# Routed experts of a two-layer mixer model: blocks of 32 places in four column groups instead of 64 in two

## What is computed

```python
N_EXPERTS = 64; TOP_K = 8; EXPERT_HIDDEN = 256; D_MODEL = 1024
def moe_ffn(t, router_w, router_bias, w1, w3, w2, sw1, sw3, sw2):
    scores = jax.nn.sigmoid(tf @ router_w)
    _, idx = lax.top_k(scores + router_bias, TOP_K)
    gate = ROUTED_SCALE * gate / jnp.sum(gate, -1, keepdims=True)
    ...
    def expert_block(acc, blk):
        tok, g, e = blk
        xb = t_ext[tok]
        hb = jax.nn.silu(xb @ w1[e]) * (xb @ w3[e])
        return acc.at[tok].add((hb @ w2[e]) * g[:, None]), None
    ...
    shared = (jax.nn.silu(tf @ sw1) * (tf @ sw3)) @ sw2
    return acc[:n_tok] + shared
```

## Time and profile before

| | us |
|---|---|
| median of 3 runs | 2253.8 (2253.52 to 2259.19) |
| the profiled execution, its own time | 2257.79 |
| its span, first to last instruction | 2256.0 |
| routed experts of layer 0 on PE | 624.3 to 1204.5 |
| routed experts of layer 1 on PE | 1661.7 to 2201.1 |

### The profile page before, as it was taken

How to read it: one execution, slowest core, us unless ns; L and a number is a source line. 1 busy time by engine, 2 the same in 40 slices (tenths; PEclk the granted TensorE clock), 3 DMA queues, 4 the chain that set the end, 5 groups by cost and what they waited for, 6 DMA issues and landing times. The chain is left out here.

```text
span 2256.0 us, 31768 instructions
## 1 busy us (share of the span) xinstructions
PE 1924.1 (85%) x10720; PEld 984.6 (44%) x10721; DVE 847.4 (38%) x1771; ACT 287.6 (13%) x566; POOL 655.2 (29%) x948
## 2 busy tenths in 40 slices
PE   6999988976799989999996797696689878877894
PEld 2333344734455445555553333244455444443442
DVE  0224458834623223333331737433443222222224
ACT  2123354112000000000001200201100000000001
POOL 1000000000356546666661000000056444434430
PEclk9999999998799999999998899798799999989997
DMA  8655410131489999989993560405369999999935
GB/s 353 259 213 215 170 39 0 68 158 50 194 338 411 412 414 404 388 339 411 388 365 163 231 233 28 186 0 220 130 255 408 413 413 413 413 412 410 408 137 205
DMA packets 99717, 601.65 MB, mean 267 GB/s; under 512 B 23120, under 2 KB 23227, under 8 KB 40188
## 3 DMA queue, kind: packets, MB, share of 16 engines
q1 hardware_dynamic: 64396, 499.67, 54.6%
q0 software_dynamic: 35248, 100.98, 12.1%
HBM read 590.50 MB, written 51.92 MB: 285 GB/s over the span
## 5 line engine op out<-in xcount | busy, mean ns | idle before, releaser
L1737 PE MATMUL bank<-moe_w,blk_xT 128*64 128x256 f32 x5632 | 683.7, 398 | 0.0
L1737 PEld LDWEIGHTS bank<-moe_w,blk_xT 128*64 128x64 f32 x5632 | 406.7, 143 | 219.7 <-issue 33.4
L1748 PE MATMUL bank<-moe_w,xt 128*64 128x512 f32 x1408 | 332.1, 592 | 1.5 <-DVE xt L1825 1.5
L1664 POOL DMA_INDIRECT ada_rows<-v_tokens,blk_gidx x264 | 272.5, 1032 | 140.8 <-issue 135.4
L1813 DVE STREAM_TRANSPOSE blk_xT<-ada_rows 128x512 f32<-128x512 f32 x132 | 94.0, 712 | 454.3 <-PE bank L1737 434.6
L494 PE MATMUL bank<-moe_w,xt 128*128 128x512 f32 x544 | 246.2, 609 | 14.0 <-DMA moe_w<-in_odd_w_in 9.7
L1680 POOL DMA_INDIRECT y_rows<-xt,blk_sidx x176 | 180.0, 1023 | 96.5 <-issue 53.8
L1796 ACT ACTIVATE xt<-bank 128x128 f32<-128x128 f32 x174 | 48.3, 278 | 1057.3 <-PE bank L1737 1057.3
L1832 DVE COPY xt<-bank 128x512 f32<-128x512 f32 x176 | 121.8, 692 | 149.3 <-PE bank L1748 149.3
L494 PEld LDWEIGHTS bank<-moe_w,xt 128*128 128x128 f32 x544 | 104.0, 195 | 150.3 <-issue 138.5
L1748 PEld LDWEIGHTS bank<-moe_w,xt 128*64 128x64 f32 x1408 | 101.1, 137 | 127.4 <-issue 100.5
(11 more groups left out here) (382 smaller groups left out, 1651.6 us busy)
## 6 DMA issues: line engine op xcount, KB each, us to landing
moe_w<-in_experts SPq DMA_DIRECT2D x128, 3072.0 KB, 31.5
moe_w<-in_ada_w POOLq DMA_DIRECT2D x20, 2048.0 KB
moe_w<-y_rows SPq DMA_DIRECT2D x24, 1024.0 KB, 20.2
moe_w<-in_even_w_in SPq DMA_DIRECT2D x8, 2048.0 KB, 8.5
moe_w<-in_odd_w_in SPq DMA_DIRECT2D x7, 2048.0 KB, 12.6
moe_w<-in_ada_w SPq DMA_DIRECT2D x4, 2048.0 KB, 14.5
ada_rows<-v_tokens,blk_gidx POOLq DMA_INDIRECT x264
moe_w<-in_even_w_out SPq DMA_DIRECT2D x1, 4096.0 KB, 13.8
```

The lines of the kernel that those rows point to most:

```text
L1664: pool.indirect_dma_start(came[q][:, u], None, v_quarters, bass.IndirectOffsetOnAxis(ap=gidx[q][:, u:u + 1], axis=0), bounds_check=4 * n_t ...
L1737: last = nc.tensor.matmul(g.bank[1][64 * h:64 * h + 64, 0:HID], xT[:, k], w[:, s, (2 * k + h) * HID:(2 * k + h + 1) * HID], start=k == 0, ...
L1748: last = nc.tensor.matmul(g.bank[3][64 * h:64 * h + 64, :], hT[:, 64 * m:64 * m + 64], w[:, s, at:at + 512], start=m == 0, stop=m == 1)
```

## The change

Blocks have SB = 32 places. The 128 partitions now hold four quarters of 32 places each, in the gathered tile as in the result.

- `up_project` runs 8 x 4 = 32 matmuls: stationary 128x32, moving 128 columns, in four column groups. `down_project` runs 2 x 4 = 8: stationary 128x32, moving 256 columns. The weights are laid out for this on the host; their size is the same.
- `hidden` is 128x64, and DVE turns it in 32x32 squares straight into `hT`; the transpose on PE and the copy from bank 2 are gone. PE has a wait with a semaphore increment in its place.
- A block has one gather (128 rows of 1 KB) and one scatter (128 rows of 1 KB). Both take their row numbers from the two columns of one tile `places`, which DVE fills (`list_places`, one copy of 128x2 each turn); POOL copies nothing.
- DEPTH is 6: six `came`, `y` and `places` tiles, and the total of blocks is rounded up to a multiple of 6. Scatters run LAG = 3 blocks behind. From the counts: 161 blocks, run as 162, in layer 0, and 100, run as 102, in layer 1: 264 turns.
- `routing_stage` compares with 32 slots instead of 64 and with 192 block numbers instead of 128 (layer 1: 126 for 96), and lays out one list instead of three.

```diff
-SB = P // 2
-DEPTH = 4
+SB = P // 4
+DEPTH = 6
...
+LAG = 3
...
-                    for u in range(2):
-                        pool.indirect_dma_start(came[q][:, u], None, v_quarters, bass.IndirectOffsetOnAxis(ap=gidx[q][:, u:u + 1], axis=0),
-                                                bounds_check=4 * n_tok - 1, oob_is_err=False).then_inc(gathered[q], 16)
...
+                    pool.indirect_dma_start(came[q], None, v_quarters, bass.IndirectOffsetOnAxis(ap=places[q][:, 0:1], axis=0),
+                                            bounds_check=4 * n_tok - 1, oob_is_err=False).then_inc(gathered[q], 16)
+
+                def next_gather(b, q):
+                    pool.wait_ge(xt_ready, b + 1)
...
+                    gather(b + DEPTH, q)
...
-                    pool.indirect_dma_start(y_halves, bass.IndirectOffsetOnAxis(ap=sidx[q][:], axis=0), y[:, q], None,
-                                            bounds_check=2 * TOPK * n_tok - 1, oob_is_err=False).then_inc(stored[q], 16)
...
+                    pool.indirect_dma_start(y_quarters, bass.IndirectOffsetOnAxis(ap=places[(q + LAG) % DEPTH][:, 1:2], axis=0), y[:, q], None,
+                                            bounds_check=4 * TOPK * n_tok - 1, oob_is_err=False).then_inc(stored[q], 16)
...
-                def turn_hidden(b):
-                    pe.wait_ge(hidden_done, b + 1)
-                    nc.tensor.transpose(g.bank[2][:, 0:P], hidden, g.ident).then_inc(hid_turned, 1)
...
-                        for h in range(2):
-                            last = nc.tensor.matmul(g.bank[1][64 * h:64 * h + 64, 0:HID], xT[:, k],
-                                                    w[:, s, (2 * k + h) * HID:(2 * k + h + 1) * HID], start=k == 0, stop=k == KT - 1)
+                        for q in range(4):
+                            at = (4 * k + q) * P
+                            last = nc.tensor.matmul(g.bank[1][SB * q:SB * q + SB, 0:P], xT[:, k], w[:, s, at:at + P],
+                                                    start=k == 0, stop=k == KT - 1)
...
-                        for h in range(2):
-                            at = W13 + m * D + h * 512
-                            last = nc.tensor.matmul(g.bank[3][64 * h:64 * h + 64, :], hT[:, 64 * m:64 * m + 64],
-                                                    w[:, s, at:at + 512], start=m == 0, stop=m == 1)
+                        for q in range(4):
+                            at = W13 + m * D + q * DQ
+                            last = nc.tensor.matmul(g.bank[3][SB * q:SB * q + SB, 0:DQ], hT[:, SB * m:SB * m + SB], w[:, s, at:at + DQ],
+                                                    start=m == 0, stop=m == 1)
...
-                    turn_hidden(before)
+                    pe.wait_ge(hidden_done, before + 1)
+
+                    pe.sem_inc(hidden_met, 1)
                     up_project(before + 1, s)
                     down_project(before, s_before)
...
+                def list_places(p, q, cols=slice(0, 2), again=True):
+
+                    b = DEPTH * p + q
+                    if again:
+                        dve.wait_ge(stored[(q - LAG) % DEPTH], 16 * (p + (q - LAG) // DEPTH))
+
+                        dve.sem_inc(rows_met, 1)
+                    nc.vector.tensor_copy(places[q][:, cols], r["places"][:, bass.ds(b + DEPTH, 1), cols].rearrange("p b u -> p (b u)")).then_inc(listed, 1)
...
-                def copy_hidden(b):
-                    dve.wait_ge(hid_turned, b + 1)
+                def turn_hidden(b):
+                    dve.wait_ge(hidden_done, b + 1)
 
                     dve.wait_ge(y_done, b)
-                    nc.vector.tensor_copy(hT, g.bank[2][:, 0:P]).then_inc(hid_ready, 1)
+                    nc.vector.transpose(hT, hidden).then_inc(hid_ready, 1)
```

176 lines of the change are left out of this document (86 added, 90 removed).

## The result

The changed kernel takes 2436.7 us, median of four runs (2429.7 to 2443.4), against 2256.5 us (four runs, 2253.5 to 2263.9) for the kernel before: a ratio of 1.078, 95% interval 1.0745 to 1.082. The prediction said 2221 us with a range to 2272, so it has the wrong sign.

A forecast was written before the change was run, and what follows sets the result against it. Weights were taken to bound layer 1 and layer 0's start, PE the middle of layer 0. Gains of 24 us (layer 0) and 12 (layer 1) took 2257.8 to 2222, at the median 2221 us; chance 0.45, range 2206 to 2272.

The forecast's parts named there:

- The turn: PE's step between up-projections of one expert: 2.85 us instead of 5.58, including a wait for `hidden`.
- first turn: An expert's first block on PE: 3.88 us, as register reads and the wait for weights are no longer hidden under queued MATMULs.
- Layer 1: Expert stage bound by weights: gain of 12 us, nearly all after the last weights land, 2 from an earlier stream start.
- Layer 0: Expert stage: gain of 24 us, with PE's turns and the weights' floor each at 528 us.
- The walk over the experts: Layer 0 stepped through 64 experts with their counts, weight loads and PE turns: ends at 1169 instead of 1195.
- Rival 2: PE's six-expert loop, 2070 instructions (129 KiB), no longer held: layer 0 gains 12 us instead of 24; 2233 us, chance 0.22.
- How many reads: Rival 2's count of instruction fetches in layer 0: one piece at each of 8 jumps back.
- What one costs: Rival 2's price of a 16 KB instruction piece at a jump back: 2.5 to 3 us.
- Rival 1: PE not fed fast enough: at 20 ns an instruction, up-projection 2.56 us, turns 3.7 and 4.6; 2350 us, chance 0.20.
- Rival 3: Gap ahead of the up-projection 0.3 us longer per turn: layer 0 +10, layer 1 -9; 2254 us, chance 0.13.
- What is hidden: POOL's gather and scatter (2.63 us), DVE's work (1.4 us) fit in a 2.85 us turn; DMA scatters taken as 0.

The follow-up runs named there:

- short code: Changed kernel, six places, TensorE's code written once per expert with a branch (about 1300 instructions): 2238.0 us (0.990) on a fast chip, 2454.1 (1.079) and 2470.6 (1.085) on slow ones.
- the version with one read: Short code with one register read instead of two at the first turn of five in six experts: 2222.6 us (0.983) on a fast chip, 2448.2 (1.078) on a slow one.

## Why the prediction was wrong

**The turn: right.** 2.85 us for a further turn, measured 2.85 to 2.96; up-projection 1.69 us of weight loads, as worked out; turning x 0.446 and silu 0.223, within 0.01; multiply 0.18 against 0.20; first turn 3.88, measured 3.93 in layer 0 away from the jump back. The last agreement has some luck in it: the working that is given for 3.88 (the wait reached 1.8 us after the last MATMUL instead of 0.9) comes to 3.76. So has the 0.27 us for a semaphore and PE's steps, which had no row behind it and measures 0.28.

**Layer 1: right in its size, once the code fits, and half right in its source.** The sum gave 12 us, nearly all of it behind the last weights; the short code's stage is 518.7 us against 530.3, which is 11.6. Of these, 5.7 lie behind the last weights (from their landing to the last turning of x it is 10.3 us instead of 16.0) and 5.8 ahead of it (the stream ends 508.5 us after the first turning, not 514.2), where 2 had been counted. That the total fits is luck in part.

**Layer 0: the direction right, the size too large.** The sum gave 24 us; short code gives 8 (569.9 against 577.9), with first turns at 4.2, and 18 with first turns at 3.4, which is less than the 3.88 that the sum had. The walk over the experts seems to have been too kind to a run of short experts: in the version with one read PE still waits 34 us for weights ahead of 10 up-projections. Of the 22 us that the sum called waits for weights in the kernel before, its trace shows 15.7 as such. That this version takes 2223 us on a chip of the fast kind, beside a forecast of 2221, is luck in part: it is another kernel, its two stages give 18 + 12 of the 36 us, and the rest lies outside them.

**Rival 2: the step that failed.** The forecast put nothing for reading the loop's code again ("the loop's code no longer stays in PE" had a chance of 0.22), and the rival that had the term priced it at 12 us. It measures 194 us. The rival's mechanism is what happened, and the signs that the prediction named for it are there: 65 instruction reads from 720 to 1170, and PE idle at every sixth expert. Layer 0's stage ends at 1320 (its last turning of x), not before 1190. The runs show loops of 1110, 1300 and 1380 instructions held, of 2070 and more not, and one of 1730 held in one stage and not in the other. The Trainium skill ("Runtime: NRT & Kernel Launch", section "Instruction fetch mechanics") states room for 2048 instructions of PE, first in, first out, in blocks of 16 KiB; the loops of 1110 to 1380 and of 2070 and more agree with that, and the loop of 1730 in layer 1 does not. Three numbers of the rival were wrong.
- *How many reads.* It had one piece per jump back, 8 of them. All pieces of the loop are read in every iteration, ten each time and 180 more than before in all. That is what one would see if the newest piece displaced the oldest: the beginning of the loop is gone when it jumps back, and each piece that is read displaces the one needed next. No run tests that order by itself.
- *What one costs.* It took 2.5 to 3 us from a small transfer on a quiet queue, once per jump. The jump back takes 6.3 us in the median and up to 7.7, and the stops are up to 8.2 and 9.3 us; the turn at the jump back has a median of 12.0 us in layer 0 and 14.0 in layer 1, where the ordinary first turns have 3.9 and 7.0. Per extra read it comes to 194 us / 175 = 1.1 us for the changed form and 158 us / 180 = 0.9 for the kernel before, both with what the lower clock costs.
- *Layer 1.* It "has room", the rival said, as the weights bound it. But weights are only asked for when PE is done with a place. A PE that stops delays the next loads, and the idle time of the stream is not made up: DMA fell from 0.93 over this stage to 0.87, and the layer lost 68 us instead of gaining.

With these sizes, which are known only now, the rival would have stood at about 2221 + 180 x 0.9 = 2383, still 54 us short. Its cost was taken at one small value and never bounded from above, although no row showed such a read with PE waiting; and a trace that shows no more than 69 KB held gave no reason to prefer "129 KiB is held" (0.45) to "it is not" (0.22).

**Rival 1: absent on one kind of chip, real on the other.** On the fast kind 64 weight loads pass in 1.69 us and nothing is held up. On the slow kind it is the largest single cost, further turns of 4.5 to 4.6 where the rival had 3.7, in time with GpSimd's issues, which no text had thought of. **Rival 3**: a gap longer by 0.1 at most. **What is hidden**: GpSimd's 2.63 us of 2.85 fit on the fast kind, as said, and the list copy, in the undisturbed turn above, holds nobody up.

## What to carry to other kernels

Count the instructions of a loop body per engine before making its work finer: halving TensorE's matmuls in size doubles the code, and once the body passes what is held (here between 1380 and 2070 instructions of 64 bytes, with 1730 held in one place and not in another) every iteration reads all of it again, here at about 1 us of time for each 16 KB, also in a stage that the weights bound. The sequencer's branch at the jump back says it in one row of the trace: 6.3 us instead of 0.2. Written once with a branch in place of two copies, the same kernel went from +7.7% to -1.0%, and with a register read spared to -1.7%. Compare two kernels only in the same set of runs on the same chip: this pair differed by 8% in three sets of runs and by 15% in a fourth, and the version with short code was 1% faster than the kernel before in one and 8% slower in two.

## What the runs showed of the hardware

- The pieces of a loop that is too long are read while weights fill the DMA engines. The branch that jumps back takes 6.3 us in the median where it took 0.21 in the kernel before, and PE stops for up to 9.3 us; the two packets of the branch shown above moved for 0.9 and 1.6 of its 6.9 us.
- The same loop of about 1730 instructions was read again in layer 1 (108 reads) and not in layer 0 (18), in three runs of three.
- On the chips of three of six sets of runs each indirect DMA issue of GpSimd goes with 0.6 to 1.3 us more for a turn of TensorE that otherwise works through 160 instructions in 2.85 us: 2.85 us beside no issue, 4.54 beside two. That the issue is the cause is argued. With the kernel before, which needs half as many instructions per turn for twice the time, the slow kind shows little (2271 to 2278 us against 2256 to 2263).
- In undisturbed turns the MATMULs on the four column groups start 12, 7 and 7 ns apart and the next four some 85 ns later, eight instructions in 110 ns.
